# A two-layer GLA/SSD decoder step: the residual's base copies go out at the residual task of their own step, and one chunk load is issued earlier

## The reference

```python
def trunk(x, ...):
    for i in range(DEPTH):                      # DEPTH = 2
        h = rmsnorm(x, pre_norm[i])
        if i % N_MIXERS == 0:
            y, S = gla_mixer(h, ...)            # in-projection, chunked scan, gate, out-projection
        else:
            y, S, buf = ssd_mixer(h, ...)
        x = x + rmsnorm(y, post_norm[i]).astype(x.dtype)
    return x, ...
```

## Time and profile before

| | us |
|---|---|
| executions | 1636.64, 1643.12, 2970.75 |
| median | 1643.12 |
| the profiled execution | 1636.64 |
| its span in the trace | 1634.9 |
| TensorE matmul, busy | 1518.6 |
| VectorE, busy | 1186.8 |
| ScalarE, busy | 824.5 |
| GpSimd, busy | 238.6 |

### The profile page before, as it was taken

One profiled execution on the slowest core, in us unless ns is written; L12 is line 12 of the kernel. 1 busy time (PEld: TensorE's weight loads), 2 busy tenths in 40 slices (PEclk: granted clock), 3 DMA queues, 4 the chain that ended last, 5 costly groups with the idle time before them and its releaser, 6 DMA issues. The chain is left out here.

```text
span 1634.9 us, 26150 instructions
## 1 busy us (share of the span) xinstructions
PE 1518.6 (93%) x8970; PEld 1266.4 (77%) x8970; DVE 1186.8 (73%) x2587; ACT 824.5 (50%) x1835; POOL 238.6 (15%) x427
## 2 busy tenths in 40 slices
PE   6989999899999979898999999889989999999876
PEld 5979777667878869898888888767777778778654
DVE  4556477957786887868887798876769676587665
ACT  4634343445455545546664664544546364554441
POOL 5010112001220200112110220210002110000002
PEclk8999999999999999999999999999999999999998
DMA  6454454344565533448855765743675765556641
GB/s 172 135 156 117 133 148 144 106 138 141 150 156 174 149 114 100 130 111 204 230 141 127 228 167 129 216 121 83 190 189 139 180 166 138 163 142 158 149 142 58
DMA packets 312095, 242.60 MB, mean 148 GB/s; under 512 B 32760, under 2 KB 283452, under 8 KB 311804
## 3 DMA queue, kind: packets, MB, share of 16 engines
q1 hardware_dynamic: 302140, 208.28, 47.3%
q0 software_dynamic: 9824, 32.64, 7.3%
HBM read 180.40 MB, written 64.97 MB: 150 GB/s over the span
## 5 line engine op out<-in xcount | busy, mean ns | idle before, releaser
L1377 PE MATMUL bank<-h,w 128*128 128x268 f32 (+1 forms) x4752 | 840.8, 331 | 32.7 <-ACT w L805 28.0
L1377 PEld LDWEIGHTS bank<-h,w 128*128 128x128 f32 x4752 | 704.4, 192 | 110.6 <-issue 41.2
L790 PE MATMUL bank<-s_w_out,s_yt_hi 128*128 128x512 f32 (+1 forms) x576 | 186.6, 405 | 15.7 <-DVE s_w_out L821 6.9
L819 DVE TENSOR_TENSOR w<-w_raw,w 128x1024 fp32r<-128x1024 f32 x132 | 160.9, 1219 | 52.5 <-ACT w L805 52.1
L805 ACT ACTIVATE w<-w_raw 128x1024 fp32r<-128x1024 f32 x132 | 138.7, 1051 | 37.7 <-DMA w_raw<-in_ssd_w_in_dram 37.2
L790 PEld LDWEIGHTS bank<-s_w_out,s_yt_hi 128*128 128x128 f32 (+1 forms) x576 | 103.0, 183 | 46.5 <-issue 8.9
L1455 DVE SCALAR_TENSOR_TENSOR conv<-before_conv,cw,conv 128x260 f32<-128x260 f32 (+2 forms) x216 | 125.2, 580 | 4.3
L790 PE MATMUL bank<-s_w_out,s_yt_lo 128*128 128x512 f32 (+1 forms) x288 | 115.3, 400 | 0.0
L790 PE MATMUL bank<-g_w_out,g_ot_hi 128*128 128x512 f32 (+1 forms) x288 | 100.5, 431 | 0.0
L2210 ACT ACTIVATE s_decay<-s_decay,t_ac 128x128 f32<-128x128 f32 (+1 forms) x288 | 85.4, 379 | 1.2
L1857 DVE COPY_PREDICATED g_attn<-g_lmask,bank 128x128 f32<-128x128 int32 (+1 forms) x208 | 60.6, 291 | 33.8 <-PE bank L1839 25.7
(11 more groups left out here) (230 smaller groups left out, 2513.8 us busy)
## 6 DMA issues: line engine op xcount, KB each, us to landing
w_raw<-in_ssd_w_in_dram SPq DMA_DIRECT2D x80, 512.0 KB, 4.2
w_raw<-in_gla_w_in_dram SPq DMA_DIRECT2D x48, 512.0 KB, 4.2
s_decay<-kept_acd SPq DMA_DIRECT2D x32, 512.0 KB, 8.4
w_raw<-in_ssd_w_out_dram SPq DMA_DIRECT2D x32, 512.0 KB, 4.3
g_chunk<-kept_gq SPq DMA_DIRECT2D x32, 448.0 KB, 5.0
s_chunk<-kept_sq SPq DMA_DIRECT2D x32, 384.0 KB, 4.9
kept_sq<-stage SPq DMA_DIRECT2D x80, 134.0 KB, 4.2
kept_sq<-stage SPq DMA_DIRECT2D x40, 256.0 KB, 4.6
```

The lines of the kernel that those rows point to most:

```text
L790: last = pe.matmul(bank[0:n, :], yt[a][:, k, 0:n], wo[:, k, b, 512 * half:512 * half + 512], start=(k + a + b == 0), stop=(k == tiles - 1 ...
L819: dve.tensor_tensor(self.part(i, 1), self.raw(i), hi, ALU.subtract).then_inc(self.w_lo, 1)
L1377: last = pe.matmul(bank[:, 0:n], w[:, p.tile % 2, a, k, :], h[:, b, k, c:c + n], start=(i == 0), stop=(i == len(terms) - 1))
```

## The change

`first_rows(s)` of layer 0 is no longer a task of its own in head block 2. SyncE calls it in `residual`, at the task "r_in" of the same step in head block 3, for steps 0 to 8. In the list `between` the chunk load (1, ("load", 1)) stands right behind (1, ("load", 0)), in front of "r_in" of step 8 and of the fill of pieces. Nothing else is changed.

```diff
@@ Plan.skeleton
-        between = [(0, ("turn", 0)), ("fill", 0.5), (0, ("products", 0)), (1, ("load", 0)),
-                   (0, ("r_add", -1)), (0, ("r_out", -1)), (0, ("r_in", 0)), ("fill", 0.8), (0, ("r_square", 0)), (1, ("load", 1)),
+        between = [(0, ("turn", 0)), ("fill", 0.5), (0, ("products", 0)), (1, ("load", 0)), (1, ("load", 1)),
+                   (0, ("r_add", -1)), (0, ("r_out", -1)), (0, ("r_in", 0)), ("fill", 0.8), (0, ("r_square", 0)),
                    (1, ("decay", 0)), ("fill", 0.5), (1, ("inputs", 0)), ("fill", 0.8), (0, ("r_add", 0)),
                    (0, ("r_out", 0)), ("fill", 0.7)]
@@
-                if L == 0 and u == U - 2:
-                    tasks.append(("base", s))
@@ program, block.sync
-            elif name == "base":
-                rows.first_rows(sp, *at)
             elif name == "r_in":
                 rows.residual(sp, *at)
@@ Rows
     def residual(self, sp, L, s):
         if (L, s) in ((0, 0), (0, 5), (1, 1)):
             self.weight_run(sp, "r", L, group_of(s))
-        if self.added_here(L, s):
+        if L == 0:
+            self.first_rows(sp, s)
+        elif self.added_here(L, s):
             self.load_residual(sp, L, s)
```

## The result

The changed kernel takes 1646.64 us (median of 20 runs, 1642.86 to 1653.56), the kernel before 1637.45 us (20 runs, among them the one of 2970.75, which hardly moves the median). The ratio is 1.0051 [1.0039, 1.0062]: the change costs 8 to 9 us, half a per cent. That is within 2% and inside the predicted range of 1630 to 1650, but it is not the "no change" that was forecast: the interval leaves 1 out.

The account below looks back on a forecast made before the run. TensorE, busy 93% of the span, was taken to bound the kernel, so only its gaps count. Removal, new place of the copies and swap (+6.5 - 6.5) summed to 0 + 0 + 0 on 1639.9: 1640 us, range 1630 to 1650.

Parts of the forecast that it names:

- TensorE bounds, and only its gaps count: TensorE is busy 93% of the span; a change counts only through its gaps and the slow clock behind them.
- The removal from unit 2: Taking eight 512 KB copies out of unit 2, where no wait is for a transfer: 0, at most 6.2 us gained.
- copies 0 to 7 into unit 3: Copies issued at "r_in" in unit 3 make no accumulation wait: 0, bound 4 us in all.
- D: Unit 3: the moved copies cost up to 4 us there, 1644 us; chance 0.07.
- E: Unit 2: the copies cost time there and their going is a gain, 1633.8 us; chance 0.07.
- F: Around 745 us: nothing happens, as issues there wait for something else, 1640 us; chance 0.52 together with A.
- The chain of the new gap: Around 750 us: late store 143 delays piece 146's tanh, then rounding; 4.2 us gap before piece 150, old gap before 765 filled.
- The length of the burst: SyncE's queue from 741.96: 1798 KB at 135 KB a microsecond take 13.3 us, so store 143 lands at 755.3.
- The slow stretch of 2.3 us behind the gap: After a TensorE gap the clock is 0.50 for 5 us, 23 matmuls instead of 42, costing 2.3 us.
- A: Edge of the layers: the trade, a new gap replaces the old one, 1640 us; chance 0.52 together with F.
- B: Store 143 lands before 750 and 145 earlier than now, the gap at 761 closes, 1633.5 us; chance 0.17.
- C: Store 143 lands later than 755.3, up to +4.5 us: 1644.5, with a second slow stretch 1646.8 us; chance 0.17.

Follow-up runs that it names:

- e1: The changed kernel with chunk load (1, 0, 1) back at its old place, so only the copies have moved; 0.9994 [0.9982, 1.0005] of the kernel before.
- e3: The changed kernel with four stage buffers instead of three; 1.0031 [1.0012, 1.005] of the kernel before.
- e5: The changed kernel with only the 384 KB chunk of load (1, 0, 1) moved forward, decays and gate at the old place; 1.0003 of the kernel before.
- e12: The kernel before with chunk load (1, 0, 1) moved, decays in 4 KB runs and GpSimd's sample loads behind step 8's accumulation; 0.9906 of the kernel before.
- e10: The kernel before with chunk load (1, 0, 1) moved and GpSimd's three sample loads behind step 8's accumulation; 1.0015 [0.9994, 1.0036] of the kernel before.

## Why the prediction was wrong

**TensorE bounds, and only its gaps count.** Right: busy times unchanged, the loss is a gap and the slow clock behind it.

**The removal from unit 2, priced at 0, and copies 0 to 7 into unit 3, at 0.** Both right. e1 has them alone, 0.9994 [0.9982, 1.0005], and the waits of 285 to 350, 583 to 650 and 395 to 500 us are as they were. The tightest copy, that of step 4, is issued at 467.29 and its accumulation at 483.91, 2.7 us earlier than before, like all around it; GpSimd nowhere waits for a copy. Rivals D (1644) and E (1633.8) fall with e1, and F, nothing at all, with the trace of after.

**The chain of the new gap.** Right in each link: three chunk transfers and the copy in front of the store, ScalarE's tanh of piece 146 waiting for it, the rounding behind, the gap before piece 150, a clock of 0.50 behind that, and the old gap filled. e3 shows the link through the stage buffer by taking it away.

**The length of the burst.** This is the step that failed: "I scale the same burst ... so 135 KB a microsecond", 1798 KB, 13.3 us, so the store lands at 755.3. It was 18.4 us. The start was right: 739.74 in a trace that runs 2.4 us ahead is 742.1 in the time of before, and I had 741.96. So the store landed at 760.5 in that time, 5.2 us later than predicted, and the gap was 4.2 + 5.2 = 9.4 (measured: 9.37). It was the duration alone.

By the landings of the changed kernel the burst divides like this (each row from the landing of the one above it):

| landed | priced at 135 KB/us | measured |
|---|---|---|
| chunk, 384 KB | 2.8 us | 5.8 us |
| decays, 512 KB | 3.8 us | 7.5 us |
| gate, 256 KB | 1.9 us | 2.4 us |
| copy 8, 512 KB | 3.8 us | 1.1 us |
| store of 143, 134 KB | 1.0 us | 1.5 us |

The copy was priced too high, what stands in front of it too low. One reason is where the rate was taken. Windows of the old burst in the kernel before, then of the new one in the changed kernel, and the packets of its first microseconds (740 to 743):

```profile
745.07:759.40 14.33, 14.33 (x118) 13.01 (x117) 9.98 (x28) 7.82 (x25) 4.93 (x10) 1.00 1.07 276
...
739.74:743.00 3.26, 3.26 (x29) 3.26 (x28) 3.19 (x10) 2.23 (x7) 0.85 (x1) 1.00 0.48 66
743.00:758.10 15.10, 7.33 (x60) 6.81 (x58) 3.52 (x13) 4.08 (x17) 4.01 (x9) 0.88 0.96 259
...
DMA packets 1606, 0.16 MB, mean 53 GB/s; under 512 B 1599, under 2 KB 1605, under 8 KB 1606
```

The swap puts the load right behind chunk load (1, 0, 0), whose decays are 1024 pieces of 96 bytes, and for 3.3 us all queues together move 66 GB/s. The kernel before has such a stretch too (740.95 to 745.07, 109 GB/s), but it ends where the burst begins from which the rate was taken. As an estimate, the 215 KB of these 3.3 us would go in 0.8 us at 259 GB/s, so the slow start costs some 2.4 of the 5.1 us by which the burst is longer than predicted. No run took it away: e5 and e12 begin with 69 GB/s as well. Behind it the rate is 6% lower than in the old burst. GpSimd's accumulation of step 7 is at work in that time, but it is in the old burst too.

The runs give prices of single terms. They overlap (GpSimd's loads are partly in the second row) and do not add up to the burst:

| term in the burst | priced at 135 KB/us | measured |
|---|---|---|
| copy 8, 512 KB | 3.8 us | 1.6 us (18.4 - 16.8) |
| decays and gate, 768 KB | 5.7 us | 8.0 us (18.4 - 10.4) |
| of it: decays in 1024 pieces and not 128 | not priced apart | 2.3 us (16.8 - 14.5) |
| GpSimd's sample loads | held to be in the average, and in both bursts | 2.9 us (16.8 - 13.9) |

The errors of the first two rows cancel: 9.6 us for the 9.5 priced. The excess is in the rest, chunk and store, 518 KB: 18.4 - 9.6 = 8.8 us for 3.8 priced, if the rows may be taken together; the slow start lies in this part.

What is left in e12, 11.6 us, has beside the chunk load the small chunk load (1, 0, 0) ahead, with pieces shorter than 512 bytes, and GpSimd's accumulation of step 7. Neither was taken away in a run, so their shares stay open.

**The slow stretch of 2.3 us behind the gap.** It was 3.5 (the prediction's 42 and 23 matmuls are not all "of the same kind", but durations bear the 3.5 out as well): after a gap of 9.4 us the clock stood at its lower level through 760 to 765 us and for a part of 765 to 770 (mean 0.70). Term for term: + (9.37 + 3.5) in the place of + (4.2 + 2.3), and - 6.5 for the old gap, as predicted. Sum + 6.4 in the place of 0.

**The rivals.** A, the trade, was the forecast and did not hold in size. It would nearly have held without copy 8 and with GpSimd's loads out of the way: e10 has a gap of 4.79 and a ratio of 1.0015 [0.9994, 1.0036]. B, the early store, was wrong, and with it the estimate from the Trainium skill ("DMA: Bandwidth & Descriptors", section "Anatomy of one DMA — SWDGE (gpsimd) path", its fit for one DMA): 6.2 us for what took 18.4, in this trace of a full queue. C, a later store, was the case that came, by its mechanism and in its place; its bound, the slowest transfer of the old burst, 11.3 us, was too low (12.4 us for the store, 14.5 for the gate), and the upper end of its 1644.5 to 1646.8 counted on an old gap that opens again, which it did not. The measured cost, 8 to 9 us, is more than its 4.5 to 6.8. That the measured 1646.64 us is nearly its 1646.8, and inside the range, is luck: the prediction counts from 1640, and the kernel before takes 1637.45. C's argument, "GpSimd's loads come in the same microseconds", is true (2.9 us by e10), but they are in the old burst as well; the argument that was missing is the slow start.

## What to carry to other kernels

Before a small store is put behind large loads in one queue, look whose buffer it frees, and price each transfer ahead of it by its own kind (the trace has a landing for each) and by the other queues' work of the same microseconds, and not by a mean rate. A rate is that of its stretch: this burst was moved out of the stretch in which the rate was read, into one with 66 GB/s. A trade of two gaps of one size is only even while the new wait is exactly as long as the old; where its length is a transfer's landing, its error goes straight into the time. Where a queue is the bottleneck, look for a load that moves few GB/s at a high DMA share: here a small table read by all partitions from one place, which fewer and longer pieces made faster (0.9906), more than any order of the same transfers gave.

## What the hardware showed unexpectedly

- The same 512 KB took 4.2 us to land as a weight tile, 8.4 us as decays in pieces of 512 bytes, 6.5 us as decays in runs of 4 KB. The Trainium skill ("DMA: Bandwidth & Descriptors", section "Specifications") gives 512 bytes as the least transfer for line rate. The trace agrees for the chunk, 340 GB/s in such pieces, and not for the decays, which all partitions read from one place, 117 to 144 GB/s; for them longer runs were worth 0.94% of the kernel.
- A DMA share near 1 is not a rate: 340 GB/s at 1.12 and 117 GB/s at 0.90 stand three microseconds apart in one trace.
- A DRAM to DRAM copy of 512 KB in the middle of a burst lands 12.6 us after its issue and lengthens the burst by 1.6 us.
- GpSimd's accumulating DMA of 512 KB has the DMA engines nearly to itself from 745 to 747 us of the changed kernel: 207 to 210 GB/s at a share of 1.03 to 1.05.
- Eight copies of a table that many partitions read made the kernel slower (1.0043 against 0.9906 with one): the load ran on some 8 DMA engines and not on 16, at 141 to 160 GB/s and not at 376.
